# Low parts of half the plain down-projection weights made by an accumulating transfer

## The reference

```
def half_ffn(h, l, j):
    y = swiglu(rms_norm(h, ffn_norm_pre[l, j]), ffn_w_gate[l, j], ffn_w_up[l, j], ffn_w_down[l, j])
    return h + 0.5 * rms_norm(y, ffn_norm_post[l, j])
def swiglu(x, w_gate, w_up, w_down):
    return (jax.nn.silu(x @ w_gate) * (x @ w_up)) @ w_down
```

## Time and profile before

| | |
|---|---|
| runs | 2312.73, 2313.27, 2313.78 us |
| span of the profiled execution | 2311.2 us; the profile shows no other total for it |
| median less span | 2.1 us |
| TensorE | 2289.0 us of matmuls, 99% of the span |
| DVE, ACT, POOL | 58%, 42%, 3% |
| granted clock of TensorE | 0.997 |

### The profile page before, as it was taken

The page is one execution under the profiler, slowest core; times in us unless marked ns, Lnnn a source line. Parts: engine busy times, 40 slices in busy tenths (PEclk is TensorE's granted clock), DMA queues, the critical chain, the costliest instruction groups (busy, mean ns, idle before and its releaser), DMA issues. The chain is left out here.

```text
span 2311.2 us, 30089 instructions
## 1 busy us (share of the span) xinstructions
PE 2289.0 (99%) x11883; PEld 1940.0 (84%) x11883; DVE 1336.2 (58%) x1862; ACT 977.3 (42%) x1612; POOL 73.6 (3%) x115
## 2 busy tenths in 40 slices
PE   8999999999999999999999999999999999999998
PEld 7888888888888888888888888888878888888887
DVE  5857536596645646573355564346897574557334
ACT  5433324444444444443343433235266554444332
POOL 0000003000000000000010000000000000000000
PEclk9999999999999999999999999999999999999999
DMA  4332332311223223413323313333322222341321
GB/s 168 108 130 79 95 110 74 109 64 55 74 74 105 70 78 105 146 59 105 98 85 119 124 59 102 106 95 92 101 74 83 92 65 92 110 135 48 117 93 73
DMA packets 171650, 217.70 MB, mean 94 GB/s; under 512 B 13080, under 2 KB 123000, under 8 KB 171512
## 3 DMA queue, kind: packets, MB, share of 16 engines
q1 hardware_dynamic: 171400, 215.75, 29.0%
q10 hardware_dynamic: 112, 0.03, 0.0%
HBM read 213.63 MB, written 2.10 MB: 93 GB/s over the span
## 5 line engine op out<-in xcount | busy, mean ns | idle before, releaser
L2111 PE MATMUL ps<-xlo,whi 128*128 128x512 f32 (+1 forms) x2056 | 755.5, 367 | 2.1 <-DVE wlo L1324 2.1
L2112 PE MATMUL ps<-xhi,wlo 128*128 128x512 f32 (+1 forms) x2056 | 753.2, 366 | 0.0
L2113 PE MATMUL ps<-xhi,whi 128*128 128x512 f32 (+1 forms) x2056 | 753.0, 366 | 0.0
L1324 DVE SCALAR_TENSOR_TENSOR wlo<-raw,vec,whi 128x512 fp32r<-128x512 f32 (+1 forms) x488 | 340.8, 742 | 388.9 <-ACT whi L795 387.8
L795 ACT ACTIVATE whi<-raw,vec 128x512 fp32r<-128x512 f32 (+1 forms) x488 | 320.8, 709 | 445.4 <-PE ps L2113 390.5
L2111 PEld LDWEIGHTS ps<-xlo,whi 128*128 128x128 f32 x2056 | 388.6, 189 | 65.6 <-issue 2.7
L2113 PEld LDWEIGHTS ps<-xhi,whi 128*128 128x128 f32 x2056 | 388.4, 189 | 62.9
L2112 PEld LDWEIGHTS ps<-xhi,wlo 128*128 128x128 f32 x2056 | 388.6, 189 | 62.0
L1319 DVE TENSOR_TENSOR wlo<-raw,whi 128x1024 fp32r<-128x1024 f32 x104 | 126.7, 1223 | 183.1 <-ACT whi L791 182.3
L791 ACT ACTIVATE whi<-raw 128x1024 fp32r<-128x1024 f32 x104 | 109.5, 1057 | 199.7 <-PE ps L2113 199.3
L2111 PE MATMUL ps<-wlo,xhi 128*128 128x512 f32 x352 | 138.6, 394 | 1.0 <-issue 1.0
(11 more groups left out here) (291 smaller groups left out, 2909.5 us busy)
## 6 DMA issues: line engine op xcount, KB each, us to landing
raw<-ffn_w_gate_dram SPq DMA_DIRECT2D x176, 256.0 KB, 2.8
raw<-ffn_w_up_dram SPq DMA_DIRECT2D x176, 256.0 KB, 3.1
raw<-ffn_w_down_dram SPq DMA_DIRECT2D x96, 256.0 KB, 3.1
w<-ffn_w_down_dram SPq DMA_DIRECT2D x72, 256.0 KB, 5.3
raw<-xattn_w_kv_dram SPq DMA_DIRECT2D x64, 256.0 KB, 2.9
raw<-even_w_in_dram SPq DMA_DIRECT2D x56, 256.0 KB, 2.9
raw<-odd_w_in_dram SPq DMA_DIRECT2D x42, 256.0 KB, 2.9
raw<-xattn_w_q_dram SPq DMA_DIRECT2D x32, 256.0 KB, 3.0
```

What stands on the lines that cost most here:

```text
L1324: last = v.scalar_tensor_tensor(out=lo[:, k, :], in0=full[:, k, :], scalar=vec[:, c:c + 1], in1=hi[:, k, :].bitcast(f32), op0=MUL, op1=SUB)
L2111: mm(out_ap, lh, rl, start=start, stop=False, skip_group_check=skip_group_check)
L2112: mm(out_ap, ll, rh, start=False, stop=False, skip_group_check=skip_group_check)
L2113: return mm(out_ap, lh, rh, start=False, stop=stop, skip_group_check=skip_group_check)
```

## The change

In the stages `down`, the pieces with an odd number in their column group (p1, p3, p6 and p8; 16 in the kernel) get their low part in another way. ACT writes `-raw` into `wlo`, in the short format, ahead of its copy of `raw` to `whi`; POOL, after `hi_made`, issues one transfer of 512 KB from the weight in DRAM that adds to what stands in `wlo`; DVE does no subtraction, but copies one column as a mark, so that `lo_made` is still counted in order (it frees the slot of `raw`); TensorE waits for `lo_made` and for the transfer's own semaphore, one for each of the four slots.

```diff
+    slot_marks = place("slot_marks", [P, SPLIT_SLOTS])
...
+    raw_added = [sem(f"raw_added{i}") for i in range(SPLIT_SLOTS)]
...
+    by_dma = []
+    for kind, _, arg, ng, n in STAGES:
+        for g in range(ng):
+            for i in range(group_pieces(kind, g, n, arg) if kind != "quads" else n):
+                by_dma.append(kind == "down" and i % 2 == 1)
...
+    def added_before(n):
+        return sum(by_dma[m] for m in range(n % SPLIT_SLOTS, n, SPLIT_SLOTS))
...
@@ gpsimd
-            elif ends_sublayer(kind, arg) and opens_scaled(n_stage):
+            if kind == "down":
+                for g_ in range(ng):
+                    for kp in range(1, np_, 2):
+                        n = base_piece + np_ * g_ + kp
+                        slot, j = n % SPLIT_SLOTS, arg[0]
+                        k0 = (2 * FF_GROUPS[arg[1]][0] + 2 * kp) * P
+                        rows_in = A["ffn_w_down"][l, j][k0:k0 + 2 * P, columns(g_)].rearrange("(a p) n -> p a n", p=P)
+                        pool.wait_ge(hi_made, n + 1)
+                        g.dma_start(wlo[:, slot], rows_in, accum_op=ADD).then_inc(raw_added[slot], 16)
+            if ends_sublayer(kind, arg) and opens_scaled(n_stage):
@@ scalar, split(n)
+            if by_dma[n]:
+                a(flat(wlo[:, slot]), flat(raw[:, from_slot]), ACT.Copy, scale=-1.0)
@@ vector, split(n)
+            if by_dma[n]:
+                dve.wait_ge(hi_made, n + 1)
+                v.tensor_copy(slot_marks[:, slot:slot + 1], ones[:, 0:1]).then_inc(lo_made, 1)
+                return
@@ tensor, weights(n)
+            if by_dma[n]:
+                pe.wait_ge(raw_added[n % SPLIT_SLOTS], 16 * (added_before(n) + 1))
```

More of the change, by code:

```diff
@@ L453, in unit_source @@
         return {"B11": w11, "T3": w11, "B21": w21, "T4": w21, "T1": w12, "T2": w12}[name][:, q, :]
+    by_dma = []
[3 more added lines that the diff above has]
+                by_dma.append(kind == "down" and i % 2 == 1)
+    assert len(by_dma) == total_pieces
+    def added_before(n):
+        return sum(by_dma[m] for m in range(n % SPLIT_SLOTS, n, SPLIT_SLOTS))
     piece_gain = []
```

## The result

The changed kernel takes 2318.07 us (median of 8 runs, 2315.63 to 2320.43) against 2312.65 us (8 runs, 2310.36 to 2313.78): ratio 1.0027, 95% interval 1.0017 to 1.0036, which is 3.9 to 8.3 us. The forecast was 2320.5 us, slower by 0.31%.

The account below looks back on a forecast made before the run. TensorE's matmuls, 99% of the 2311.2 us span, bound the kernel. Waits at p8 of 4.8 us plus 2.4 us for sharing make 7.2: span 2318.4, with 2.1 for runs 2320.5 us; range 2312.7 to 2337.

Parts of the forecast that it names:

- Place: TensorE in the down stages: waits some 1 to 2 us each, all at p8; p1, p3 and p6 without a gap.
- a sign of being wrong: PE's matmuls outside the down stages: if they moved, the prediction would be wrong.
- Covered edits: ACT's sixteen 1.0 us copies, DVE's marks of at most 0.16 us, TensorE's second waits, POOL's queue: no cost.
- Window: p8 of a down stage: 5.9 us from the end of ACT's two copies to first use, for issue and transfer.
- Transfer alone: POOL's accumulating 512 KB: issue 0.9 us plus transfer 6.2 us, taken from plain 1024 KB, together 7.1 us.
- Sharing: SP's next load beside p8's transfer: 0.8 us in three stages, bounds 0 and 1.65 us.
- Sum: p8 late by 1.2 us in four stages and 0.8 more in three: 7.2 us added to the span.
- The transfer fits: Rival at p8: issue and transfer take up to 5.9 us, no new wait, time 2313.3 us; chance 0.36.
- POOL is held up by DVE: Rival at p8: POOL stands still for DVE's four multiplications, 2.5 us later, 17.2 us in all, 2330.5 us; chance 0.12.
- The addition is not slow enough: Rival of a slow addition: landing takes say 16 us, p1, p3 and p8 late, 63 us, 2376 us; chance 0.07.
- Faster: Rival: DVE, 17 us freer, ends a wait elsewhere, at most 2.1 us; chance of more than that 0.02.
- Clock: TensorE: a wait of a few microseconds costs no clock, as the granted clock is 1.00 in the first 20 us.

Follow-up runs that it names:

- the early issue: The changed kernel, but POOL waits only for ACT's negated copy, not the high part behind it: 2312.56 us, ratio 1.0000 against the kernel before.
- both edits: The changed kernel with POOL issuing after the negated copy and SP's load into p8's raw slot held until p8's transfer landed: 2312.94 us, ratio 1.0004.
- p9: The changed kernel with p9 made by a transfer as well, 20 in all: 2345.7 us, ratio 1.0145 against the kernel before.

## Why the prediction was right

- *Place.* The forecast said that p8 alone would be late. The two kernels that split the pieces show it: 1.0001 without p8, 1.0029 with p8 alone. That the profile would name the transfer as the releaser was wrong; it writes "issue". Matmuls outside the four stages moved too, by some 2 us in the first mixer, which the prediction had named as a sign of being wrong. The kernel with p8 alone has the same waits and a granted clock of 0.98 there, above the 0.95 of before, so the move does not follow from the waits.
- *Covered edits.* ACT's copies, DVE's marks (0.15 us each) and TensorE's further waits cost nothing, as said: with twelve pieces made that way the ratio is 1.0001, and with all sixteen and the early issue 1.0000. Nor does POOL's queue.
- *Window.* Forecast 5.9 us, measured 5.6: POOL starts its issue 0.3 us after the high part's copy ends (346.34 + 1.04 = 347.38 against 347.68), which the forecast left out.
- *Transfer alone.* Forecast 7.1 us (issue 0.9, transfer 6.2), measured 5.8 with the issue in it. The step that took the 1024 KB row for an accumulating 512 KB was too long by about 1.3 us. The packets take longer with the addition (3.2 against 1.9 us), which fits a second read and does not prove it. But the 1024 KB row also writes 1024 KB, and its 6.2 us is the middle of two transfers of 4.9 and 7.5 us that ran among the other loads of the start. The interpolation for plain 512 KB, 4.1 us, passed over rows of that size in the same trace: `post_gain` lands in 3.7 to 5.7 us over SP's queue. POOL's plain transfer took 3.6.
- *Sharing.* Forecast 0.8 us in three stages, half of what the load takes; measured 1.3 to 1.8, about all of its 1.65.
- *Sum.* Forecast waits of 2.0, 2.0, 2.0 and 1.2 us; measured 1.85, 1.93, 1.55 and 0.26. In the first three stages a transfer priced 1.3 us too long stands against a window 0.3 us too wide and a sharing about 0.8 us too small, and the errors nearly cancel. That those three waits came out so close is luck; the fourth, where nothing is shared, shows it: a fifth of what was forecast. The place and the kind of the wait were not luck.
- *Rivals.* "The transfer fits" is what a microsecond earlier makes of it (1.0000). "POOL is held up by DVE" falls with the multiplications left out. The addition is not slow enough for p1 or p6 to be late. "Faster" falls with the kernel that has both edits.
- *Clock.* That a wait would cost no clock held for the waits at p8, 1.9 us at most, behind which the matmuls soon have their distance of 0.23 us again. As a general statement it was wrong, as p9 shows, where the wait is 4 us and more. Nor did the row under it carry it, the granted clock of 1.00 in the first 20 us. There the same matmul starts 0.21 us after the one before up to 16.8 us, and 0.12 us from then on. In the changed kernel's trace the window shows 0.50 for such a stretch. Before, in the two stretches, and then after:

```profile
16.35 0.41 PE L2112 MATMUL ps<-xhi,wlo 128*128 128x256 f32 x1
16.56 0.38 PE L2113 MATMUL ps<-xhi,whi 128*128 128x256 f32 x1
...
16.90 0.28 PE L2112 MATMUL ps<-xhi,wlo 128*128 128x256 f32 x1
17.02 0.28 PE L2113 MATMUL ps<-xhi,whi 128*128 128x256 f32 x1
```
```profile
13.40:16.80 3.40, 3.40 (x19) 3.40 (x18) 2.91 (x5) 3.40 (x7) 0.00 (x0) 0.50 1.03 390
```

The Trainium skill's fixed 2.0 us plus bytes over 436 GB/s (DMA: Bandwidth & Descriptors, section Anatomy of one DMA) gives an estimate of 3.2 us for 512 KB. The plain transfer from POOL took 3.6 us alone, near that; the accumulating one took 5.8. With 1024 KB put in, the same figures of the Trainium skill give an estimate of 4.4 us. By either p8 would not have waited where nothing is shared; in the fourth stage it waited, by 0.26 us.

## What to carry to other kernels

When the bound engine never waits, moving work off another engine can only keep the time or add to it; look first for the piece with the shortest time between "slot free" and "first use", and price the new path against that window, not against the mean. A step moved earlier elsewhere (here the mark that frees a load slot) may start a transfer just when the new one needs the engines. Putting the new path's start on the first thing that it needs (the negated copy) was worth more than the microsecond it saved.

## What the runs showed of the hardware

An accumulating transfer of 512 KB issued from POOL landed after 5.6 to 5.9 us when alone and mostly after 7 to 9 us beside SP's loads; without the addition it took 3.6 us alone. At p8 of the first stage, where it overlaps with SP's load, it landed after 5.8 us with its own packets first and after 7.3 us with SP's first. Waits of TensorE of up to 2.4 us (with p8 alone) left the granted clock at 1.00; those of 4.1 to 5.3 us were followed by 0.50, in the first stage for 5.6 us.

Part of the scatter between executions may come from the clock in the first mixer, which no kernel here changes. From 500 to 600 us it was 0.93 in the changed kernel's profiled run, the slowest of its eight with 2320.43 us, and 0.98 in that of the kernel with p8 alone, the fastest of its seven with 2315.34 us. These are two kernels, with one profile each, so that it makes the scatter of one kernel is not shown:

```profile
500.00:600.00 100.00, 99.88 (x658) 87.49 (x656) 66.56 (x78) 42.64 (x73) 3.83 (x1) 0.98 0.18 59
```
